# Expert loop of a decoder layer: which engine's queue issues the two down-projection weight chunks

## The reference, cut to what matters

```python
def expert_ffn(xe, wgu, bgu, wd, bd):
    gu = xe @ wgu + bgu                      # 1024 -> 2048
    gate = jnp.minimum(gu[..., :D_EXPERT], SWIGLU_LIMIT)
    up = jnp.clip(gu[..., D_EXPERT:], -SWIGLU_LIMIT, SWIGLU_LIMIT)
    glu = gate * jax.nn.sigmoid(gate * SWIGLU_ALPHA)
    return ((up + 1.0) * glu) @ wd + bd      # 1024 -> 1024
...
logits = (xf @ w_router + b_router).astype(jnp.float32)
top_v, top_e = lax.top_k(logits, TOP_K)
top_w = jax.nn.softmax(top_v, axis=-1)
```

## Time and profile before

| | |
|---|---|
| Median of 3 timed runs | 1904.99 us (1904.98 to 1905.03) |
| Profiled execution | 1906.55 us, its span 1904.8 us |
| TensorE busy | 1776.2 us, 93% of the span |
| ScalarE busy | 297.5 us, 16% |
| VectorE busy | 568.0 us, 30% |
| Mean DMA rate over the span | 256 GB/s; 405 to 419 GB/s in the slices of the expert loop |
| Expert loop | from about 915 us to 1889 us of the span |

### The profile page before, as it was taken

The page is one execution under the profiler, slowest core; times in us unless marked ns, Lnnn a source line. Parts: engine busy times, 40 slices in busy tenths (PEclk is TensorE's granted clock), DMA queues, the critical chain, the costliest instruction groups (busy, mean ns, idle before and its releaser), DMA issues. The chain is left out here.

```text
span 1904.8 us, 25092 instructions
## 1 busy us (share of the span) xinstructions
PE 1776.2 (93%) x9128; PEld 882.0 (46%) x9128; DVE 568.0 (30%) x1470; ACT 297.5 (16%) x727; POOL 34.0 (2%) x87
## 2 busy tenths in 40 slices
PE   6999997979899997998999999999999999999997
PEld 3776555546678886655333333333333333333332
DVE  3201215446623333113232222223132222323223
ACT  0111312114433332000110101011010101011011
POOL 2000001000000000001000000000000000000000
PEclk9999997756779998996999999999999999999998
DMA  5233316124032330806799999999999999999993
GB/s 184 95 126 133 119 40 139 52 72 148 23 84 66 107 104 17 235 0 252 280 405 416 418 411 413 416 410 419 407 419 414 409 417 410 418 408 419 406 419 116
DMA packets 144953, 487.98 MB, mean 256 GB/s; under 512 B 18381, under 2 KB 63313, under 8 KB 112079
## 3 DMA queue, kind: packets, MB, share of 16 engines
q1 hardware_dynamic: 144544, 486.43, 66.5%
q10 hardware_dynamic: 366, 0.99, 0.2%
HBM read 480.24 MB, written 11.28 MB: 258 GB/s over the span
## 5 line engine op out<-in xcount | busy, mean ns | idle before, releaser
L1818 PE MATMUL bank<-wring,ex_xe 128*64 128x512 f32 x2048 | 453.6, 595 | 0.0
L1818 PEld LDWEIGHTS bank<-wring,ex_xe 128*64 128x64 f32 x2048 | 141.4, 137 | 306.0 <-issue 306.0
L1892 DVE TENSOR_TENSOR acc<-acc,bank 128x512 f32<-128x512 f32 (+1 forms) x198 | 124.0, 680 | 507.1 <-PE bank L1795 506.4
L1841 PE MATMUL bank<-wring,ex_atT 128*64 128x512 f32 x1024 | 226.8, 595 | 0.0
L317 PE MATMUL bank<-uT,w_slots 128*128 128x320 f32 x512 | 138.1, 433 | 0.0
L1841 PEld LDWEIGHTS bank<-wring,ex_atT 128*64 128x64 f32 x1024 | 70.7, 137 | 133.3 <-issue 127.9
L1795 PE MATMUL bank<-ex_ys,ex_oht 64*128 64x512 f32 x396 | 102.8, 624 | 17.7 <-DVE acc L1892 16.9
L317 PEld LDWEIGHTS bank<-uT,w_slots 128*128 128x128 f32 x512 | 97.2, 190 | 40.9 <-issue 0.5
L1863 ACT ACTIVATE ex_oht<-bank 128x320 f32<-128x320 f32 x32 | 14.0, 438 | 597.1 <-PE bank L1826 597.1
L1778 PE MATMUL bank<-xn,ex_oh 128*64 128x512 f32 (+1 forms) x396 | 98.9, 618 | 2.8 <-DVE ex_oh L1881 2.8
L1915 DVE TENSOR_SCALAR ex_gt<-bank 128x512 f32<-128x512 f32 x32 | 22.1, 692 | 184.2 <-PE bank L1818 184.2
(11 more groups left out here) (451 smaller groups left out, 1721.0 us busy)
## 6 DMA issues: line engine op xcount, KB each, us to landing
wring<-w_gu SPq DMA_DIRECT2D x128, 2048.0 KB, 12.4
wring<-w_dn SPq DMA_DIRECT2D x64, 2048.0 KB, 10.8
w_slots<-w_in SPq DMA_DIRECT2D x13, 2048.0 KB, 7.8
ns_pa<-cache_kv SPq DMA_DIRECT2D x64, 192.0 KB, 2.5
state_ce<-state_C SPq DMA_DIRECT2D x8, 512.0 KB, 7.8
new_C_s<-state_ce SPq DMA_DIRECT2D x4, 1024.0 KB
ns_pb<-cache_kv SPq DMA_DIRECT2D x64, 64.0 KB, 1.9
w_branch<-w_branch_m SPq DMA_DIRECT2D x4, 1024.0 KB, 10.2
```

The costliest lines, as they stand in the source:

```text
L1818: last = pe.matmul(half(2 + gu, h), xe[:, k % 4, k // 4, :], m.wring[:, k // 2, o:o + H], start=False, stop=(k == KD - 1))
L1841: last = pe.matmul(half(4, h), atT[:, k % 4, k // 4, :], m.wring[:, 4 + k // 4, o:o + H], start=(k == 0), stop=(k == 7))
L1892: dve.tensor_tensor(part, part, m.bank[(6, 4, 6)[r // 2] + r % 2][0:n, :], ALU.add).then_inc(s_acc, 1)
```

## The change

In the loop the loads of chunks 4 and 5 are taken out of SyncE's program and put into ScalarE's, at the end of the turn, behind the copy of `ex_ys`. `weight_loads` now takes the list of chunks. ScalarE reads the next item's expert from `etab` into a register and issues both loads with no wait of their own: the wait for `s_used` at 6 i + 6 ahead of the copy covers both. The last turn has no next item, so it is written out behind the loop without the loads. The first item's six loads in `route` stay with SyncE, and so do the waits and loads of chunks 0 to 3 in the loop. The computation is the same.

```diff
--- before.py
+++ after.py
@@ -1493,9 +1493,9 @@
                 dve.scalar_tensor_tensor(m.xn[0:rows, t, :], m.x[0:rows, t, :], rstd, m.g2[0:rows, :], ALU.mult, ALU.mult)
 
 
-def weight_loads(sp, m, a, e, wait=None):
-
-    for c in range(NCHUNK):
+def weight_loads(sp, m, a, e, chunks, wait=None):
+
+    for c in chunks:
         if wait is not None:
             wait(c)
         if c < 4:
@@ -1553,7 +1553,7 @@
                 sp.dma_start(m.bgu[gu * NE:(gu + 1) * NE, :], a.b_gu[0, :, gu * FE:(gu + 1) * FE]).then_inc(s_bg, 16)
             for h in range(2):
                 sp.dma_start(m.ys[h * SLOT:h * SLOT + NE, :], a.b_dn[0, :, h * (D // 2):(h + 1) * (D // 2)]).then_inc(s_c2, 16)
-            weight_loads(sp, m, a, 0)
+            weight_loads(sp, m, a, 0, range(NCHUNK))
             sp.wait_ge(s_bg, 32)
             sp.wait_ge(s_c2, 32)
 
@@ -1766,7 +1766,7 @@
             with sp.Fori(1, nw) as i:
                 e = sp.value_load(m.etab[0:1, bass.ds(i, 1)], min_val=0, max_val=NE - 1)
 
-                weight_loads(sp, m, a, e, wait=lambda ch: sp.wait_ge(s_used, NCHUNK * i + (ch + 1 - NCHUNK)))
+                weight_loads(sp, m, a, e, range(4), wait=lambda ch: sp.wait_ge(s_used, NCHUNK * i + (ch + 1 - NCHUNK)))
 
         @block.tensor
         def _(pe):
@@ -1857,7 +1857,8 @@
             copy(xg[:, :], 0, s_xg)
             act.wait_ge(s_xT, 1)
             copy(flat(xe), 0, s_xe)
-            with act.Fori(0, nw) as i:
+
+            def turn(i, more):
                 act.wait_ge(s_tr, i + 1)
                 act.wait_ge(s_sc, 6 * i + 6)
                 act.activation(oht[:, 0:NTOK], m.bank[1][:, 0:NTOK], ACT.Copy).then_inc(s_oht, 1)
@@ -1871,6 +1872,13 @@
                 copy(flat(xe), 0, s_xe)
                 act.wait_ge(s_used, NCHUNK * i + NCHUNK)
                 copy(ys[:, :], 4, s_ys)
+                if more:
+                    e = act.value_load(m.etab[0:1, bass.ds(i + 1, 1)], min_val=0, max_val=NE - 1)
+                    weight_loads(act, m, a, e, range(4, NCHUNK))
+
+            with act.Fori(0, nw - 1) as i:
+                turn(i, True)
+            turn(nw - 1, False)
 
         @block.vector
         def _(dve):
```

## The result

The changed kernel takes 1925.19 us (1920.77 to 1929.38, four runs) against 1904.99 us; as a ratio 1.0108, with an interval of 1.0084 to 1.0132. The forecast was no change, with a range to 1918. A second set of runs gave 1925.35 us against 1903.46, ratio 1.0110 (1.0095 to 1.0125). The profiled execution took 1920.77 us, the shortest of the four; its span is 1919.0.

A forecast was written before the change was run, and what follows sets the result against it. TensorE was taken to bound the expert loop, with transfers just keeping up; removed SyncE issues, added ScalarE work and later loads were worth 0 + 0 + 0, so the median stays 1905.0 us (68%), range 1903.5 to 1918.

The forecast's parts named there:

- What bounds the kernel: Expert loop: TensorE sets the 30.42 us turn; transfers keep up at 413.7 GB/s with almost nothing to spare in rate.
- The added work on ScalarE: Behind the ex_ys copy: register load and two issues, 1.6 us a turn, hidden in 18.66 us idle before ex_oht; worth 0.
- The late issue: Chunk 4 issued 3.9 to 4.6 us later, chunk 5 0.9 to 2.1 us later, both still landing before their need.
- The other chunks: Gate/up chunks land up to 4.6 us later, 19.6 us against 26.6 until use, 7.0 us of lead left; worth 0.
- The step that failed: Down projection: chunks 4 and 5 land early by 11 and 11.5 us at the worst, from landings of 9.4 to 13.1.
- Rival A: Down projection: ScalarE's and SyncE's rings share unevenly, chunk 5 comes late; slower, 1911 or 1918 us by form; chance 17%.
- row-by-row form: Rings alternate row by row, ScalarE gets a third: 7.5 us stall once, then 0.2 us a turn, 1918 us; chance 10%.
- rows 11: Trace rows of the kernel's start: SyncE's ring moved 184 packets while ScalarE's moved none; later 664 small beside 41 large.
- the form that I had priced: Rings alternate in larger blocks of equal row counts: only a first stall of some 6 us, 1911 us; chance 7%.
- Rival B: Loop transfers: mixing two rings lowers the DMA rate; a 2% loss gives 1913 us, 4% costs 26 us; chance 8%.
- Rival C: SyncE's ring goes first, chunk 5 behind all four gate/up chunks: 7 us a turn, some 2110 us; chance 3%.
- Rival D: Descriptors of both engines worked off in issue order, rings act as one: same time as forecast, part of its 68%.

The follow-up runs named there:

- the run with one ring: Changed kernel, but SyncE issues both down chunks again, only after the ex_ys copy has ended: 1904.71 us against 1903.97, ratio 1.0005.
- 16384-byte pieces: Changed kernel with down chunks loaded in pieces of 16384 bytes and strided transpositions, run twice (one labelled 8192): 1907.13 us and 1906.91 us.
- the last run: Changed kernel with the register load and both DMA issues ahead of the ex_ys copy instead of behind it: 1903.89 us, beside 1925.35 for the changed kernel.
- 2048-byte pieces: Changed kernel with each down chunk loaded by two DMAs of half its columns: 2116.55 us, ratio 1.112.

## Why the prediction was wrong

**What bounds the kernel** held. The turn without waits is 30.42 us in both, and the transfers are the second limit.

**The added work on ScalarE** held. The two issues took 0.40 us each, chunk 4 left 0.75 us behind the start of the `ex_ys` copy (1250.36 to 1251.11; forecast 1.1), so the register load ran beside the copy, and the idle time before `ex_oht` is unchanged:

```profile
1269.61 0.44 ACT L1864 ACTIVATE ex_oht<-bank 128x320 f32<-128x320 f32 x1 [18.66 <-PE bank L1826]
```

**The late issue** held, as the run with one ring showed: 4 us later at no cost. The other chunks kept their lead as well: in the changed kernel their longest landing was 17.2 us, against the 19.6 allowed for.

**The step that failed** is "With these, chunk 4 is early by 11 us and chunk 5 by 11.5 us at the worst". It took landings measured in one ring, 9.4 to 13.1 us, for a transfer that now shares with another ring. The landing of chunk 5 became 22 to 29 us. Rival A had the mechanism, the price (8 to 29 us in its row-by-row form; measured 20, though from other parts, as said below) and even the threshold, 44% of the engines with ScalarE, but I gave it 17%, 10 of them for its row-by-row forms, because I read rows 11 as "it isn't row by row".

That reading was wrong. In 2.5 to 4.5 us of the start ScalarE's single rows (others were issued at 1.67 and 1.97, behind that of 1.40) did wait while SyncE's ring moved 184 pieces. Those are spread over the DMA engines, and a few single rows are not two rings filled on each, so the delay says little on how they share; why it came no run here shows. And of the 664 packets beside 41 nearly all were 32 bytes, while only 26 of the 41 carried data, 25 of them rows of 3264 bytes, at a moment when ScalarE's transfer was nearly over; a count over all engines says nothing where the rings aren't both filled on each. The shape of the pieces, 4096 against 8192, was known and should have had the greater weight, the more so as the sum in the row-by-row form ended at 23.1 us against 22.8, on the edge. As to the Trainium skill's rule (page "DMA: Bandwidth & Descriptors", section "Queues, rings and completion order"), that an engine goes round between its queues by packets: the going round agrees with this case's traces. Blocks of 9 to 17 descriptors do not agree with the counts of 17 to 18 in the first half microsecond, and in the form that I had priced they were to cost 6 us once, where 20 were lost all along the loop.

**Smaller errors in rival A.** The one stall of 7.5 us at the beginning did not come: the first three turns had no wait and the longest wait was 3.2 us. The loss a turn was 0.6 us (18.4 in 31 turns), near the upper bound of 0.7 and not the 0.2 that I took. That the total fell into rival A's span is therefore partly luck. The stall came from 10.1 x 3 = 30 us, as if SyncE's ring were filled from the first moment; but the first landings of chunk 4 are 7.8 and 8.3 us, about those of a lone load, so ScalarE's ring had the engines to itself until chunk 0 joined. And I took the 16 DMA engines for one. The landing is that of the slowest. In the turn with the 2.8 us wait, ScalarE's ring moved at most 16 pieces in the last 5 us before the landing; most DMA engines were through with it:

```profile
q1 hardware_dynamic: 264, 2.05, 98.4%
q10 hardware_dynamic: 16, 0.06, 2.9%
```

An engine that lags by 1 us when SyncE's chunk 0 joins has 1 us more of ScalarE's work to do at a third of the rate, so by this estimate it lands about 3 us later. That fits the landings of chunk 4, 7.8 to 14.6 us in the changed kernel against 7.5 to 9.5 us with 16384-byte pieces, but it was not tested apart.

**Rival B** is excluded: 414 GB/s over the loop in the last run's two rings, as in the kernel before. **Rival C** too: with larger pieces ScalarE's ring took 70%. (Its time was a slip as well: 31 turns of 7 us are 217 us, 2122 and not 2110.) **Rival D** is excluded by the piece counts: in the order of issue chunks 4 and 5 would have gone ahead of chunk 0, not beside it.

No run beats the kernel before beyond its interval. TensorE bounds the loop, and the best of the others only match it.

## What to carry to other kernels

When one of several DMA streams moves to another engine's queue, its landing times from the shared queue are void: between the queues the share of each goes with the size of its contiguous pieces, here 20, 33, 50 and 70% for 2048, 4096, 8192 and 16384 bytes beside 8192. Check the need time of the stream with the smaller pieces against its bytes over that share, and where the two are within a few microseconds, keep the stream in the old queue, issue earlier, or make its pieces larger. Behind a wait put the DMA issue first and the copy second: between the two kernels that differ in nothing else, 0.75 us here decided over 20.

## What the runs showed of the hardware that I had not expected

- The DMA engines alternate between SyncE's and ScalarE's ring by pieces (one or a very few at a time), whatever their size, over 2048 to 16384 bytes (SyncE's to ScalarE's: 239 to 239, 129 to 133, 417 to 421, 97 to 96 pieces).
- A wait of TensorE of 2.8 us was followed by about 3 us at clock 0.50, so its price was 4.3 us. The other nine waits in the same trace, of 0.3 to 3.2 us, were not: the half behind each took 3.65 us. In the repeat of the same kernel one wait of 2.14 us was followed by clock 0.51 and another of 2.13 us by 1.00. So the length of the wait alone doesn't decide it. With 2048-byte pieces, where the waits were 4.0 to 5.9 us, all 30 were followed by a slower half.
- Rows that lie behind each other for one partition came out as one piece of 16384 bytes, though the access pattern named pieces of 8192.
- A transposition on TensorE that reads every fourth or second column took 283 ns instead of 273, its weight load 209 instead of 140, and the four of a turn made it 0.09 us longer.
